# Expert weights in 2 MB units: a six-slot ring in place of a twelve-slot one

## The reference

```
g_sel  = argmax(x @ w_rg + b_rg)                # one of 4 groups
top 2 of the 8 experts in that group            # 32 experts in all
y[t] += gate * (silu(x[t] @ w_gate[e]) * (x[t] @ w_up[e])) @ w_down[e]
```

## Time and profile before

| | |
|---|---|
| median of 3 runs | 1884.71 us |
| profiled execution | 1879.8 us, of which the span from first to last instruction is 1878.2 us |
| PE busy | 1525.0 us, 81% of the span |
| DVE, ACT, POOL busy | 436.2, 218.2, 77.6 us |
| DMA over the whole span | 555.11 MB, 296 GB/s |
| experts' stage | from about 921 us to the end of the span |

### The profile page before, as it was taken

The page is one execution under the profiler, slowest core; times in us unless marked ns, Lnnn a source line. Parts: engine busy times, 40 slices in busy tenths (PEclk is TensorE's granted clock), DMA queues, the critical chain, the costliest instruction groups (busy, mean ns, idle before and its releaser), DMA issues.

```text
span 1878.2 us, 23928 instructions
## 1 busy us (share of the span) xinstructions
PE 1525.0 (81%) x9517; PEld 891.8 (47%) x9517; DVE 436.2 (23%) x1128; ACT 218.2 (12%) x499; POOL 77.6 (4%) x141
## 2 busy tenths in 40 slices
PE   6999999999998999999767676676775776857756
PEld 5777777776776666777523131131321322213211
DVE  3106664542133333011301102002020020200201
ACT  3010101012323333111300000000000000000000
POOL 1000000210001221000000000000000000000000
PEclk9999999999999899999888888688887888888888
DMA  7444243432444998635399999999999999999997
GB/s 251 136 132 121 87 142 107 140 117 68 138 148 168 370 398 298 217 109 218 154 423 421 421 420 422 422 422 422 422 422 422 422 422 422 422 422 422 422 420 294
DMA packets 157644, 555.11 MB, mean 296 GB/s; under 512 B 17091, under 2 KB 86788, under 8 KB 108100
## 3 DMA queue, kind: packets, MB, share of 16 engines
q1 hardware_dynamic: 149300, 517.83, 70.1%
q0 software_dynamic: 8272, 36.25, 5.4%
HBM read 545.32 MB, written 8.72 MB: 295 GB/s over the span
## 4 chain that ended last, share of the span: by engine, by line
PE 55%; DMA 36%; DVE 3%; SPq 3%; issue 1%; ACT 1%; DVEq 0%; POOL 0%; ACTq 0%
PE PS L1680 21%; DMA arena<-in_w_up_e_dram 18%; DMA arena<-in_w_down_e_dram 10%; PE PS L2132 7%; PE PS L2184 7%; DMA arena<-in_w_gate_e_dram 6%; PE PS L2230 3%; PE PS L2163 2%; DMA arena<-in_cache_mem_k_dram 2%; PE PS L2004 2%; SPq L635 2%; PE PS L2221 2%; PE PS L1719 1%; PE PS L2064 1%; PE PS L2021 1%
## 5 line engine op out<-in xcount | busy, mean ns | idle before, releaser
L2184 PE MATMUL PS<-arena 128*32 128x512 f32 x2048 | 326.3, 784 | 215.2 <-DMA arena<-in_w_up_e_dram 141.1
L1680 PE MATMUL PS<-arena 128*128 128x288 f32 (+1 forms) x1728 | 444.3, 406 | 3.3 <-DVE arena L1155 1.4
L1680 PEld LDWEIGHTS PS<-arena 128*128 128x128 f32 x1728 | 321.8, 191 | 96.4 <-issue 20.5
L2184 PEld LDWEIGHTS PS<-arena 128*32 128x32 f32 x2048 | 76.6, 139 | 455.6 <-issue 189.5
L2230 PE MATMUL PS<-arena 128*32 128x512 f32 x992 | 147.4, 754 | 78.4 <-DMA arena<-in_w_down_e_dram 78.4
L2132 PE MATMUL PS<-arena 128*128 128x288 f32 x512 | 130.9, 415 | 0.4 <-DVE arena L1443 0.4
L2230 PEld LDWEIGHTS PS<-arena 128*32 128x32 f32 x992 | 36.0, 134 | 183.3 <-issue 93.1
L1596 DVE TENSOR_TENSOR arena<-arena,PS 128x512 f32<-128x512 f32 x8 | 5.5, 687 | 505.5 <-PE PS L2184 505.5
L2132 PEld LDWEIGHTS PS<-arena 128*128 128x128 f32 x512 | 97.8, 193 | 32.4 <-issue 5.5
L2163 PEld LDWEIGHTS PS<-arena 128*128 128x128 f32 x768 | 89.6, 196 | 9.9 <-issue 8.4
L2163 PE MATMUL PS<-arena 128*128 128x128 f32 x768 | 92.4, 281 | 1.4 <-DVE arena L1570 1.4
(11 more groups left out here) (344 smaller groups left out, 1116.4 us busy)
## 6 DMA issues: line engine op xcount, KB each, us to landing
arena<-in_w_gate_e_dram SPq DMA_DIRECT2D x128, 1024.0 KB, 17.9
arena<-in_w_up_e_dram SPq DMA_DIRECT2D x128, 1024.0 KB, 19.3
arena<-in_w_down_e_dram SPq DMA_DIRECT2D x124, 1024.0 KB, 18.6
arena<-in_cache_fox_k_dram SPq DMA_DIRECT2D x64, 384.0 KB, 8.4
arena<-in_cache_fox_v_dram POOLq DMA_DIRECT2D x64, 384.0 KB, 6.9
arena<-in_w_in_dram SPq DMA_DIRECT2D x6, 3072.0 KB, 10.8
arena<-in_w_out_dram SPq DMA_DIRECT2D x8, 2048.0 KB, 9.0
arena<-in_w_in_dram SPq DMA_DIRECT2D x7, 2048.0 KB, 11.0
```

The costliest lines, as they stand in the source:

```text
L1680: last = pe.matmul(PS[0:m, bank, 0:w], wt[:, k, c:c + m], rhs[:, k, :], start=(k == 0), stop=(k == KC - 1))
L2184: last = pe.matmul(PS[x * SLOTS:(x + 1) * SLOTS, which, :], xgT[:, kk, x * SLOTS:(x + 1) * SLOTS], wt[:, k, :], start=(kk == 0), stop=(kk ...
```

## The change

A slot becomes 2 MB: 128 partitions of 16 KB, half of one expert's matrix. There are six of them in the same 12 MB (the views `whole`, which the other path already used). A group is still one slot for each of the four experts, so it is 8 MB; a quad has 6 groups (2 gate, 2 up, 2 down), and the ring holds one and a half. The rows of x are interleaved by halves in place of quarters to match (`by_half`), and the hidden activations are read with a stride of two in the transposes.

SP asks for a group by two pairs of slots, experts 0 and 1 and then experts 2 and 3, each pair behind a wait of its own. PE still waits for the whole group, does 64 records in place of 32, and raises `units_used` once at the end. The last group of the last quad is loaded as two halves of 1 MB per expert: the first as one piece, the second by columns. In the first quad the gather comes in two halves.

```diff
-GROUPS = 12
+GROUPS = 6
 GPQ = GROUPS - 1
-RING = 12
+RING = 6
...
-    w_gate_r = w_gate_e[0].rearrange("e (q p k) n -> e q p k n", q=4, p=P)
+    w_gate_r = w_gate_e[0].rearrange("e (q p k) n -> e q p k n", q=2, p=P)
...
+            def group_unit(g, x):
+                return whole[(g * XQ + x) % RING]
+            def load_pair(p, g, x0):
+                src = (w_gate_r, w_up_r, w_down_r)[g // 2]
+                for x in (x0, x0 + 1):
+                    sp.dma_start(group_unit(g, x).rearrange("p (k n) -> p k n", n=src.shape[4]),
+                                 src[ds(p * XQ + x, 1), g % 2].rearrange("e p k n -> p (e k) n")).then_inc(group_in[g % 3], 16)
...
             def ring_loads(p, last=False):
                 for g in range(GROUPS):
-                    if g < 2:
-                        sp.wait_ge(units_used, p * GPQ - (1 - g))
-                    elif g == 2:
-                        sp.wait_ge(yst_filled, p * 4)
-                    else:
-                        sp.wait_ge(units_used, p * GPQ + (g - 2))
-                    if last and g == GROUPS - 1:
-                        load_last_group()
-                    else:
-                        load_group(p, g)
+                    for x0 in (0, 2):
+                        if g == 0 and x0 == 0:
+                            sp.wait_ge(units_used, p * GPQ)
+                        elif g == 0:
+                            sp.wait_ge(yst_filled, p * 4)
+                        elif g > 1 or x0:
+                            sp.wait_ge(units_used, p * GPQ + (g - 1 + x0 // 2))
+                        if last and g == GROUPS - 1:
+                            load_last_pair(x0)
+                        else:
+                            load_pair(p, g, x0)
+                if last:
+                    load_last_columns()
...
-                    for q in range(4):
-                        g = 4 * which + q
...
-                        pe.wait_ge(group_in[g % 3], p * 256 + (64 * (g // 3) + 64))
-                        for k in range(4):
-                            kk = 4 * q + k
+                    for q in range(2):
+                        g = 2 * which + q
+                        if first and g == 1:
+                            gather(0, range(8, KC))
+                        pe.wait_ge(group_in[g % 3], p * 128 + (64 * (g // 3) + 64))
+                        for k in range(8):
+                            kk = 8 * q + k
...
                             for x in range(XQ):
...
                         last.then_inc(units_used, 1)
...
-                    last = pe.transpose(PS[:, 6, k * P:(k + 1) * P], hS[:, k * P:(k + 1) * P], ident[:, :])
+                    if last_pair and k >= 2:
+                        src = hS[:, k * P:(k + 1) * P]
+                    else:
+                        src = hS[:, :].rearrange("p (q f k) -> p q k f", q=2, k=2)[:, k // 2, k % 2, :]
+                    last = pe.transpose(PS[:, 6, k * P:(k + 1) * P], src, ident[:, :])
...
-            gather(0, range(4))
+            gather(0, range(8))
```

More of the change, by code:

```diff
@@ L38 @@
 QUADS = NE // XQ
-GROUPS = 12
+GROUPS = 6
 GPQ = GROUPS - 1
-RING = 12
-RING_DONE = [256 * QUADS] * 2 + [256 * QUADS - 64] + [0] * 3
+RING = 6
+RING_DONE = [128 * QUADS] * 3 + [0] * 3
 def build(nc, x_prompt, x_sample, cache_fox_k, cache_fox_v, cache_fox_logf, cache_mem_k, cache_mem_v,
@@ L60, in build @@
     w_out_d = w_out[0].rearrange("(k p) n -> p k n", p=P)
-    w_gate_r = w_gate_e[0].rearrange("e (q p k) n -> e q p k n", q=4, p=P)
-    w_up_r = w_up_e[0].rearrange("e (q p k) n -> e q p k n", q=4, p=P)
-    w_down_r = w_down_e[0].rearrange("e (q p k) n -> e q p k n", q=4, p=P)
+    w_gate_r = w_gate_e[0].rearrange("e (q p k) n -> e q p k n", q=2, p=P)
+    w_up_r = w_up_e[0].rearrange("e (q p k) n -> e q p k n", q=2, p=P)
+    w_down_r = w_down_e[0].rearrange("e (q p k) n -> e q p k n", q=2, p=P)
+    w_down_q = w_down_e[0].rearrange("e (q p) n -> e q p n", q=4)
     w_down_d = w_down_e[0].rearrange("e (k p) n -> e p k n", p=P)
@@ L193, in build, with in_halves, by_half @@
         whole = [view(o, UNIT) for o in UNIT_AT]
-        unit = [view(UNIT_AT[n // 2] + (n % 2) * (UNIT // 2), UNIT // 2) for n in range(RING)]
         YB = (0, 1, 6, 7)
         h_scaled = view(HSC, 3, D)
[L198 to L202, removed]
+        def in_halves(a):
+            return a.rearrange("t (q p k) -> t q k p", q=2, p=P)
+        def by_half(a):
+            return a.rearrange("t (q k p) -> t q k p", q=2, p=P)
         xgT = view(YT, KC, P)
@@ L530, in _ @@
             sp.dma_start(wslot[0], w_kv_d[:, :, 0:384]).then_inc(w_in_slot[0], 16)
-            sp.dma_start(g_ffn_r[:, :].rearrange("p (q k) -> p q k", q=4), g_ffn_norm[0].rearrange("(q p k) -> p q k", q=4, p=P)).then_inc(wff_in, 16)
+            sp.dma_start(g_ffn_r[:, :].rearrange("p (q k) -> p q k", q=2), g_ffn_norm[0].rearrange("(q p k) -> p q k", q=2, p=P)).then_inc(wff_in, 16)
             for n in range(3):
@@ L628, in _, with load_last_pair, load_last_columns @@
                 sp.dma_start(wo_slot[n % 3], w_out_d[:, :, n * 256:(n + 1) * 256]).then_inc(wo_in[n % 3], 16)
[L631 to L638, removed]
+            def group_unit(g, x):
[5 more added lines that the diff above has]
+                                 src[ds(p * XQ + x, 1), g % 2].rearrange("e p k n -> p (e k) n")).then_inc(group_in[g % 3], 16)
+            def load_last_pair(x0):
+                for x in (x0, x0 + 1):
+                    sp.dma_start(group_unit(GROUPS - 1, x)[:, 0:D], w_down_q[(QUADS - 1) * XQ + x, 2]).then_inc(group_in[2], 16)
+            def load_last_columns():
                 for c in range(4):
@@ L641, in load_last_group @@
                     for x in range(XQ):
-                        slot = ((GROUPS - 1) * XQ + x) % RING
-                        sp.dma_start(unit[slot][:, cols].rearrange("p (k n) -> p k n", k=1),
-                                     w_down_r[(QUADS - 1) * XQ + x, 3, :, :, cols]).then_inc(last_in[c], 16)
+                        sp.dma_start(group_unit(GROUPS - 1, x)[:, D + c * 512:D + (c + 1) * 512],
+                                     w_down_q[(QUADS - 1) * XQ + x, 3, :, cols]).then_inc(last_in[c], 16)
@@ L660, in load_first @@
+                if last:
+                    load_last_columns()
             def load_first(u):
-                src = (w_gate_r, w_up_r, w_down_r)[u // (4 * XQ)]
                 g, x = u // XQ, u % XQ
-                sp.dma_start(unit[u].rearrange("p (k n) -> p k n", n=src.shape[4]),
-                             src[x, g % 4]).then_inc(group_in[g % 3], 16)
-            for u in range(6):
+                sp.dma_start(whole[u].rearrange("p (k n) -> p k n", n=FFW), w_gate_r[x, g]).then_inc(group_in[g % 3], 16)
@@ L667, in _ @@
+            for u in range(3):
                 load_first(u)
             sp.wait_ge(wo_filled, 14)
-            for u in (6, 7):
+            load_first(3)
+            sp.wait_ge(h_added, 3 * KC)
+            for u in (4, 5):
                 load_first(u)
[L671 to L677, removed]
+            for g in range(1, GROUPS):
+                for x0 in (0, 2):
+                    if g > 1 or x0:
+                        sp.wait_ge(units_used, g - 1 + x0 // 2)
+                        load_pair(0, g, x0)
@@ L686, in expert_loads @@
                         sp.wait_ge(mg_filled, e * 4 + (2 * c - 2))
-                    for q in range(4):
-                        sp.dma_start(wg_u[c][:, 4 * q:4 * q + 4, :],
+                    for q in range(2):
+                        sp.dma_start(wg_u[c][:, 8 * q:8 * q + 8, :],
                                      w_gate_r[ds(e, 1), q, :, :, cols].rearrange("e p k n -> p (e k) n")).then_inc(unit_in[2 * c], 16)
@@ L691, in expert_loads @@
                         sp.wait_ge(mu_filled, e * 4 + (2 * c - 2))
-                    for q in range(4):
-                        sp.dma_start(wu_u[c][:, 4 * q:4 * q + 4, :],
+                    for q in range(2):
+                        sp.dma_start(wu_u[c][:, 8 * q:8 * q + 8, :],
                                      w_up_r[ds(e, 1), q, :, :, cols].rearrange("e p k n -> p (e k) n")).then_inc(unit_in[2 * c + 1], 16)
@@ L1080, in scale_rows @@
             def scale_rows(t, w):
-                act.activation(by_quarter(h_scaled[0:w, t, :]), in_quarters(h_tok[0:w, t, :]), ACT.Copy,
+                act.activation(by_half(h_scaled[0:w, t, :]), in_halves(h_tok[0:w, t, :]), ACT.Copy,
                                scale=rstd[0:w, 5 + t:6 + t]).then_inc(h_scl, 1)
@@ L1090, in pair_act @@
             def pair_act(p, last=False):
-                act.wait_ge(units_used, p * GPQ + 4)
+                act.wait_ge(units_used, p * GPQ + 2)
                 act.activation(hS[:, :], PS[:, 0, :], ACT.Silu).then_inc(pair_silu, 1)
@@ L1543, in _ @@
             dve.wait_ge(consts_set, N_CONSTS + 1)
```

(29 more changed lines are left out.)

## The result

The changed kernel takes 1985.67 us (median of 5 runs, 1981.2 to 1997.57), the kernel before 1882.9 (5 runs): 1.0558 times as long, 95% interval 1.0529 to 1.0588. The forecast was 1972 us, within 1905 to 2040. The profiled execution took 1988.86 us, its span 1987.2, which is 109.0 us more than before.

The account below looks back on a forecast made before the run. The kernel before was taken as bound by weight DMA at 422 GB/s. Later start +13.7 us, seven quad periods +68.6 us and the end sum to +87.3 us on the span, giving 1972 us, range 1905 to 2040 us.

Parts of the forecast that it names:

- The queue ahead: In the new ring, only half a group, 9.8 us of transfers, is prefetched to cover request delay and PE's 64-record burst.
- The cover of the old ring: When PE ends a group and SP asks for more, nearly two groups, up to 20 us, are still queued.
- The terms of a group: End to end of group: delay 3.0, transfer 9.8, semaphores 0.1, burst 9.2; 22.1 us against 19.6 its bytes need.
- rival C: PE's clock stays at 1.2 GHz through the whole burst: 64 records take 14.6 us, kernel 2145 us; chance 0.05.
- Rivals A and B: Prefetch covers the loop: A, longer rows pay, 1877 us, chance 0.06; B, they do not, 1891 us, chance 0.03.
- Rows: Weight loads with 16 KB rows run at 430 GB/s against 422; half a group takes 9.8 us, not 9.9.
- A quad: Four groups of 22.1 us, one of 20.0 and one of 20.9: 129.3 us, 9.8 more than before.
- the delay of a request: Both ends of a weight load together cost 3.0 us, bounds 2.4 and 3.5.
- the burst behind the scatter: In group 0, after 2.7 us of PE idling, the burst takes 8.0 us, between 7.43 and 9.2.
- The start: In the first quad, group 0 ends at 936.9 us and the gate and up groups end 13.7 us later.
- The end: Last quad: group 4 takes 22.1 us, then 35.0 us to the span's end at 1965.5; columns land beside other work.
- The sum: Whole span grows by 87.3 us, which on the median of the runs gives 1972 us.

Follow-up runs that it names:

- e3: Changed kernel with most of the expert matmuls left out, all loads and waits kept; 1883.16 us, 1.0005 times the kernel before.
- e4: Changed kernel with PE taking two experts at a time and releasing their two slots at once, same loads and slots; 1890.15 us, 1.0049 times the kernel before.
- e6: e4 with the second half of the next gather moved behind the first half group of the down matrices; 1875.59 us, 0.9969 times the kernel before.
- e7: e6 with each slot filled by two 1 MB loads with 8 KB rows; 1889.2 us, 1.0034 times the kernel before.
- e2: Changed kernel with added matmuls that nothing reads, keeping PE busy while it waits; 1946.72 us, 1.0342 times the kernel before.

## Why the prediction was right, step by step

*The queue ahead* was right, and is shown from two sides: with short bursts (e3) and with release by two experts (e4, e6) the same loads run at 416 to 428 GB/s in windows of 200 us, against 377 to 390 in the changed kernel. The cover of the old ring was put too high: when SP asks there, PE's wait for the next group (3.4 to 6.3 us) and one group behind it (9.9 us) are queued, so 13 to 16 us and not up to 20. No term of the sum used it.

*The terms of a group.* Forecast 3.0 + 9.8 + 0.1 of waiting and 9.2 of burst; measured 13.2 and 9.2, so 22.4 in place of 22.1. The clock came back within the burst as in the bursts before: 64 records took 10.0 us at most, not 14.6, and rival C falls. Rivals A and B fall with the DMA's gaps.

*Rows.* Forecast 430 GB/s, measured 429 to 430 in windows within a group, and 427 to 428 over 200 us in e6. That e7 comes so near the 14 us is partly luck of rounding: 390 MB at 430 in place of 422 GB/s would be 17 us, and at 428 it is 13.

*A quad.* Forecast 129.3 us in place of 119.5, from the end of one quad's up groups to the end of the next quad's. Measured in the same way it is (1925.12 - 1001.34) / 7 = 132.0, so 12.5 us more than before and not 9.8. Averaged over the seven periods, the four groups behind a wait took 22.5 us each (1.6 us a quad over the forecast), all of it the delay: waits of 13.3 us in place of 12.9. Group 0, behind the scatter, took 21.9 us in place of 20.9 and scattered most, 20.1 to 24.2 (in the quad shown 1068.47 - 1044.67 = 23.8): the scatter takes 10.7 us in place of 10.2, the wait behind it is 2.4 to 4.0 us, and the clock has then often fallen, so that bursts lie between 7.07 and 10.02 us. Group 4 took 20.1 us in place of 20.0. So the delay of a request was the term sized too small, and after it the burst behind the scatter.

*The start* came out 11.8 us later (forecast 13.7): group 0 ended at 935.1, not 936.9, and the other three groups took 22.1 us each, as forecast.

*The end* was too short in the forecast: it grew by 9.9 us, where my terms give 1965.5 - 1908.4 = 57.1 us behind the last up group, 5 more than the 52.2 of before. I let the columns land beside other work, and PE waited for them (timeline of the changed kernel, last quad):

```profile
1954.65 5.63 PE L2241 MATMUL PS<-arena 128*32 128x512 f32 x32 [7.61 <-DMA arena<-in_w_down_e_dram]
1960.11 1.03 PE L2253 MATMUL PS<-arena 128*32 128x512 f32 x8
1965.43 1.89 PE L2253 MATMUL PS<-arena 128*32 128x512 f32 x8 [4.29 <-DMA arena<-in_w_down_e_dram]
```

With release by two experts this end is 50.5 us (e4), so it too comes from asking late.

*The sum.* On the profiled span it is 11.8 + 87.3 + 9.9 = 109.0 us, where the forecast had 13.7 + 68.6 + 5.0 = 87.3. The mechanism was right; its price was a fifth too low.

*Clock.* The prediction did not say what share of the loss is PE's clock. Of 103 us, 39 go when PE is kept busy (e2). The forecast there was 76 to 96, with a quad of 120.7 us; a quad took 126.0, mostly since I took the delay of a request as 3 us however the queue stands, and the later start and the longer end (13.3 and 10.2 us over the kernel before) did not shrink.

## What to carry to other kernels

Size a ring by time, not by megabytes: what is asked ahead must last for the consumer's longest absence (its burst, plus any other work between two releases) and a request's delay at both ends. In the changed kernel a burst of 9.2 us and a delay of 3.4 stand against 9.8 us asked ahead: 2.8 us short, which is what a group of 22.4 us loses on the 19.6 that its bytes need. A larger unit in the same memory lengthens the burst and shortens the lead at once; if all buffers of a group are released together, splitting the loader's wait gives half a group ahead and no more until the consumer's order is split as well (1985.67 us, and then 1890.15). Longer rows pay where the DMA is kept busy: 428 GB/s against 422, and 13.6 us in all.

## What was not expected of the hardware

A queue that has run empty, or nearly so, does not start again at full rate: on the dry DMA of the changed kernel the first two microseconds ran at 246 and 213 GB/s and the following 15 at 430, and in e2, where the last transfers were still running when the request came, the rate fell to 213 behind it. There the half group landed 12.7 to 15.6 us after the end of the burst (13.8 on average), against 13.3 in the changed kernel, counted in the same way. An idle time of 2.4 to 4.0 us behind the scatter left PE's next burst at anything from 7.07 to 10.02 us.
